# A hybrid attention and state-space block: the first projections with rotations on VectorE, block copies on ScalarE and a reordered softmax

## What is computed

```python
def _compress(k, cmp_idx, pe, w1, w2):
    blk = k[:, cmp_idx] + pe[:, None, :]      # 31 overlapping blocks of 32 tokens
    return jax.nn.silu(blk @ w1) @ w2
q, kc, vc, ks, vs, kw, vw, gates, z = jnp.split(h @ w_in, splits, axis=-1)
s_c = jnp.einsum('bqgrd,bngd->bgrqn', qb, k_cmp) - slopes * (tf - cmp_center)
p_c = _masked_softmax(s_c, cmp_end <= t)      # 0 where a token sees no block
o_c = jnp.einsum('bgrqn,bngd->bqgrd', p_c, v_cmp)
```

## Time and profile before

| | us |
|---|---|
| median of 3 runs | 2048.51 (2045.93 to 2049.92) |
| the profiled execution | 2053.18 |
| its span | 2051.4 |
| busy: TensorE, VectorE, ScalarE, GpSimd | 1826.9, 1005.5, 816.8, 303.3 |
| TensorE's chain share | 66% |

### The profile page before, as it was taken

One profiled execution on the slowest core, in us unless ns is written; L12 is line 12 of the kernel. 1 busy time (PEld: TensorE's weight loads), 2 busy tenths in 40 slices (PEclk: granted clock), 3 DMA queues, 4 the chain that ended last, 5 costly groups with the idle time before them and its releaser, 6 DMA issues.

```text
span 2051.4 us, 23580 instructions
## 1 busy us (share of the span) xinstructions
PE 1826.9 (89%) x9454; PEld 1450.1 (71%) x9454; DVE 1005.5 (49%) x1694; ACT 816.8 (40%) x1348; POOL 303.3 (15%) x376
## 2 busy tenths in 40 slices
PE   3488699997996999999799999999999969999996
PEld 2366578775775787786487777887777748888885
DVE  7647845665564446434434454445544364334323
ACT  4034356763313424333425545256632443223222
POOL 1347432546000000000000000012200021111000
PEclk9789799998998999999999999999999979999998
DMA  3154231005667422321032221321122212233231
GB/s 108 47 168 144 99 98 42 12 1 157 156 157 167 132 84 92 105 95 48 21 116 78 82 83 62 100 69 61 63 82 92 83 41 93 92 103 100 85 95 59
DMA packets 79230, 183.37 MB, mean 89 GB/s; under 512 B 24449, under 2 KB 35585, under 8 KB 77329
## 3 DMA queue, kind: packets, MB, share of 16 engines
q1 hardware_dynamic: 79120, 181.87, 28.7%
HBM read 165.58 MB, written 16.25 MB: 89 GB/s over the span
## 4 chain that ended last, share of the span: by engine, by line
PE 66%; DVE 17%; ACT 8%; DMA 4%; issue 2%; POOL 2%; SPq 1%; DVEq 0%; ACTq 0%; POOLq 0%
PE bank L822 16%; PE bank L823 16%; PE bank L824 15%; DVE wlo L1720 2%; PE bank L861 2%; PE bank L862 2%; PE bank L863 2%; PE bank L1003 2%; PE bank L981 2%; ACT whi L1249 1%; POOL Ps L2473 1%; ACT Ps L1619 1%; DVE Pb L1842 1%; DVE CA L1688 1%; PE bank L842 1%
## 5 line engine op out<-in xcount | busy, mean ns | idle before, releaser
L1720 DVE TENSOR_TENSOR wlo<-wraw,whi 128x1024 fp32r<-128x1024 f32 (+1 forms) x262 | 327.5, 1253 | 344.1 <-ACT whi L1249 342.7
L822 PE MATMUL bank<-Hh,whi 128*128 128x512 f32 (+2 forms) x1136 | 461.2, 406 | 24.0 <-DVE wlo L1720 13.2
L823 PE MATMUL bank<-Hl,whi 128*128 128x512 f32 (+2 forms) x1136 | 448.6, 395 | 0.0
L824 PE MATMUL bank<-Hh,wlo 128*128 128x512 f32 (+2 forms) x1136 | 448.2, 395 | 0.0
L1249 ACT ACTIVATE whi<-wraw 128x1024 fp32r<-128x1024 f32 (+1 forms) x262 | 271.1, 1040 | 373.0 <-PE bank L824 260.1
L822 PEld LDWEIGHTS bank<-Hh,whi 128*128 128x128 f32 (+2 forms) x1136 | 215.5, 190 | 84.5 <-DVE qs L1786 11.8
L824 PEld LDWEIGHTS bank<-Hh,wlo 128*128 128x128 f32 (+2 forms) x1136 | 215.3, 189 | 48.9 <-issue 0.6
L823 PEld LDWEIGHTS bank<-Hl,whi 128*128 128x128 f32 (+2 forms) x1136 | 215.8, 190 | 47.5 <-issue 2.7
L2466 POOL TENSOR_SCALAR bs<-dist 128x256 f32<-128x256 f32 x16 | 7.3, 457 | 831.8 <-DMA dist<-in_c_dist 831.1
L822 PE MATMUL bank<-Bh,whi 128*128 128x512 f32 x256 | 103.1, 403 | 2.2 <-DVE Bl L2244 2.2
L824 PE MATMUL bank<-Bh,wlo 128*128 128x512 f32 x256 | 102.1, 399 | 0.0
(11 more groups left out here) (368 smaller groups left out, 3044.7 us busy)
## 6 DMA issues: line engine op xcount, KB each, us to landing
wraw<-in_w_o SPq DMA_DIRECT2D x24, 512.0 KB, 3.5
wraw<-in_w_bgate SPq DMA_DIRECT2D x24, 512.0 KB, 3.4
wraw<-in_w_branch SPq DMA_DIRECT2D x24, 512.0 KB, 3.5
wraw<-in_w_fg SPq DMA_DIRECT2D x22, 512.0 KB, 3.4
wraw<-in_w_fu SPq DMA_DIRECT2D x22, 512.0 KB, 3.4
wraw<-in_w_s SPq DMA_DIRECT2D x16, 512.0 KB, 4.1
wraw<-in_w_glu SPq DMA_DIRECT2D x16, 512.0 KB, 3.6
wraw<-in_w_fd SPq DMA_DIRECT2D x16, 512.0 KB, 3.5
```

The source lines that it names most:

```text
L822: pe.matmul(o, wh[:, cols], hi(k), start=k == 0, stop=False)
L823: pe.matmul(o, wh[:, cols], lo(k), start=False, stop=False)
L824: m = pe.matmul(o, wl[:, cols], hi(k), start=False, stop=k == K - 1)
L1720: dve.tensor_tensor(c.wlo[q][:, 0:n], c.raw[i % RR][:, 0:n], c.whi[q][:, 0:n].bitcast(F32), S_).then_inc(*up(DID, ("wlo", i)))
```

## The change

- The low part becomes a step of its own, `split_lo`. Up to the end of the projections it stands one use later than the high part; afterwards directly behind it.
- The norm's scale of tile k+1 stands ahead of the low part of tile k. The parameter work of the S5 preparation that stood ahead of and in the norm moves behind it (its parts 3 and 4 are now wider operations in place of many), and the two sines move from among the squares to behind the evictions of `w_kvc` 0 and 1.
- The evictions of `w_kvc` become plain copies on ScalarE. The position vector takes the unused column 31 of the blocks, goes through the same matmul, and returns as a bias in `cmp_hid`.
- Rotations run whole (128x1152 and 128x1024) and all on VectorE; GpSimd keeps memsets and the copies of `pr`. The copies to `Bd` go to ScalarE.
- Order of tiles: `w_kvc`, `w_gate`, then `w_ksw` 0 to 3, each followed by two pieces of `cmp_w1`, then `w_q` 0, 4, 1, 5, 2, 6, 3, 7, then `w_vsw`. The softmax runs per head index r as soon as tiles r and r+4 are there, in two steps (`soft_in`, `soft_out`) with ScalarE's exponential between; its mask product and its floor at 1e-30 go, and the gate is multiplied by `valid` once.
- The stores of `CA`, `K` and `WT` move to later steps. The wait for the last store of `WT` moves from GpSimd to the first writers of `pT`.

```diff
+        lows = deque()
+
+        def low(upto):
+            while lows and lows[0] <= upto:
+                i = lows.popleft()
+                out.append(("split_lo", i))
+                rawuser[i % RR] = -1
...
-                        rawuser[split % RR] = -1
+                        lows.append(split)
...
                         seen = i
+                        low(i + 1)
                         pump(i + LOOK)
+                        low(i)
+                        if not late:
+                            low(i + LOOK)
+                            pump(i + LOOK)
...
+        self.tick()
+        self.step("vecs")
+        for k in range(KT + 1):
+            if k < KT:
+                self.sq.take(("n0", k))
             self.step("norm0", k)
...
+            if k < KT:
+                self.sq.give(("n0", k))
+        self.step("pump", LOOK)
+        self.pair([("w_kvc", 0), ("w_kvc", 1)], "h0")
+        for n in range(2):
+            self.evict(("w_kvc", n))
+        self.tick(2)
+        for n in range(2, 4):
+            self.filled("w_kvc", n, 4)
+        self.filled("w_gate", 0, 4, M=48)
...
+            self.filled("w_ksw", t, 4)
+            if t == 0:
+                self.bank.take("gateT")
+                self.step("gate_t")
+                self.bank.give("gateT")
+            if t == 2:
+                self.cmp_out(0)
+            i, m = t // 2, t % 2
+            if m == 0:
+                self.bank.take(("hid", i))
+            for hf in range(2):
+                j = self.piece("cmp_w1", (i, m, hf), 0, 1024, split=False)
+                self.step("cmp_w1", i, m, hf, j)
+                self.tick()
+            if m == 1:
+                self.step("cmp_hid", i)
+                self.bank.give(("hid", i))
+        self.step("cmp_in")
+        for n, t in enumerate(self.turns):
+            self.filled("w_q", t, 2)
+            if n == 0:
+                self.cmp_out(1)
+            self.compressed(n)
         for j, key in enumerate(self.tok("w_vsw", 0, 512, 2, "h0", self.between_pieces())):
+            if j == 0:
+                self.prep_turn(3, 1)
+                self.step("store_w", 3, 1)
             self.evict(key)
-        self.drain()
         self.step("cmp_end")
+        self.step("first_over")
...
+    turns = (0, 4, 1, 5, 2, 6, 3, 7)
+
+    def filled(self, w, col, n, M=128):
...
-        for part in range(11):
+        for part in range(9):
             self.step("prep", part)
             yield
         for b in range(4):
             self.step("prep_b", b)
             yield
-            for n in range(6):
-                self.step("prep_ca", b, n)
-                yield
-            self.step("prep_neg", b)
-            if b < 3:
-                self.step("prep_in", b + 1)
-            yield
-            if b:
-                self.prep_turn(b - 1, 1)
-                yield
-            for n in range(6):
+            for i in range(2):
+                for n in range(3):
+                    self.step("prep_ca", b, i, n)
+                    if b:
+                        if n == 0:
+                            self.prep_turn(b - 1, i)
+                        elif n == 2:
+                            self.step("store_w", b - 1, i)
+                    yield
+            for n in range(3):
                 self.step("prep_w", b, 0, n)
+                if n == 1:
+                    self.step("store_ca", b)
+                    if b < 3:
+                        self.step("prep_in", b + 1)
                 yield
             self.bank.take(("kk", b))
             self.step("prep_k", b)
             self.bank.give(("kk", b))
-            yield
-            for n in range(6):
+            for n in range(3):
                 self.step("prep_w", b, 1, n)
+                if n == 2:
+                    self.step("store_k", b)
                 yield
-            self.prep_turn(b, 0)
-            yield
-        self.prep_turn(3, 1)
+        self.prep_turn(3, 0)
+        self.step("store_w", 3, 0)
 
     def prep_turn(self, b, i):
         for hf in range(2):
...
+    def compressed(self, n):
+
+        if 1 <= n <= 8:
+            t = self.turns[n - 1]
+            for a in range(2):
+                self.bank.take(("cs", t, a))
+                self.bank.give(("cs", t, a))
+            self.step("cmp_scores", t)
+        if n % 2 == 0 and n >= 4:
+            self.step("soft_out", (n - 4) // 2)
+        if n % 2 == 1 and n >= 5:
+            r = (n - 5) // 2
+            self.bank.take(("ct", r))
+            self.step("cmp_t", r)
+            self.bank.give(("ct", r))
+        if n % 2 == 1 and 3 <= n <= 9:
+            r = (n - 3) // 2
+            self.bank.take(("cq", r))
...
+    def ev_kvc(key):
+        b, n = bank(key), key[1]
+        i, gpair = n // 2, n % 2
+        src = b.rearrange("p (n q two) -> p two q n", q=8, two=2)
+        on.wait_ge(*at("tile", key))
+        on.wait_ge(*at("blk_pe", i))
+        for a in range(2):
+            for par in range(2):
+                for hf in range(2):
+                    x = copy(c.blk[i][par * 64:par * 64 + 64, hf * 8:hf * 8 + 8, :].rearrange(
+                        "p q (g n) -> p q g n", g=4)[:, :, 2 * gpair + a, 0:31], src[a * 64:a * 64 + 64, par, :, hf:hf + 31])
+        x.then_inc(*up(DID, ("blk", i, gpair), ("freed", key)))
...
     def cmp_hid(i):
+        b = bank(("hid", i))[:, 0:256].rearrange("p (m n) -> p m n", m=2)
         on.wait_ge(*at("hid", i))
-        act.activation(c.hid[:, i, :, :].rearrange("p a b -> p (a b)"), bank(("hid", i))[:, 0:256], ACT.Silu).then_inc(
-            *up(DID, ("hid_s", i), ("freed", ("hid", i))))
+        copy(c.hb[:, i, :], b[:, :, 31]).then_inc(*up(DID))
+        on.wait_ge(*now(DID))
+        for m in range(2):
+            x = act.activation(c.hid[:, i, m, :], b[:, m, :], ACT.Silu, bias=c.hb[:, i, m:m + 1])
+        x.then_inc(*up(DID, ("hid_s", i), ("freed", ("hid", i))))
 
...
+    def prep_b(b):
+        on.wait_ge(*at("Bb", b))
+        on.wait_ge(*at("Bd0"))
+        if b:
+            on.wait_ge(*at("kk", b - 1))
+        for i in range(2):
+            for h in range(2):
+                half = slice(h * 64, h * 64 + 64)
+                x = copy(c.Bd[half, i, :, h * 16:h * 16 + 16], c.Bb[half, i, :, :])
+        x.then_inc(*up(DID, ("Bd", b)))
...
-        if part == 1:
+        if part == 2:
             on.wait_ge(*at("angle"))
...
+        if k:
+            s = c.sq[plan.sq.of["n0", k - 1]]
+            hi, lo = c.moving["h0"]
+            on.wait_ge(*at("hi", "h0", k - 1))
+            dve.tensor_tensor(lo(k - 1), s, hi(k - 1).bitcast(F32), S_).then_inc(
+                *up(DID, ("lo", "h0", k - 1), ("freed", ("n0", k - 1))))
...
     def gate_t():
+        b = bank("gateT")[:, 0:192].rearrange("p (j h) -> p j h", j=4)
         on.wait_ge(*at("gateT"))
-        dve.tensor_copy(c.gate[:, :, :].rearrange("p a b -> p (a b)"), bank("gateT")[:, 0:192]).then_inc(
-            *up(DID, ("gate0",), ("freed", "gateT")))
+        on.wait_ge(*at("valid"))
+        dve.tensor_tensor(c.gate[:, :, 0:16], b[:, :, 0:16], c.valid.unsqueeze(2).broadcast_to([128, 4, 16]), M).then_inc(
+            *up(DID))
+        dve.tensor_copy(c.gate[:, :, 16:48], b[:, :, 16:48]).then_inc(*up(DID, ("gate0",), ("freed", "gateT")))
...
+    def rotated(o, x, w, n, y, i, b, step, *names):
+
+        p8 = slice(8 * b, 8 * b + 8)
+        wk = lambda m: w[:, m, 0:n, p8].rearrange("p k q -> p q k").unsqueeze(3).broadcast_to([128, 8, n, 16])
+        yk = lambda m: y[:, m, :, :].unsqueeze(2).broadcast_to([128, 8, n, 16])
+        if step == 0:
+            tt(o, yk(0), wk(i), M)
+        elif step == 1:
+            tt(x, yk(1), wk(1 - i), M)
+        else:
+            tt(o, o, x, A_ if i else S_, *names)
+
+    def prep_ca(b, i, n):
+        if n == 0 and i == 0:
             on.wait_ge(*at("Cq", b))
             if b:
                 on.wait_ge(*at("CAd", b - 1))
                 on.wait_ge(*at("kk", b - 1))
-        (o, a0, a1, op) = c.rotate(c.tA, c.pw, 9, c.Cq, 0, c.CA[:, 0, :, :, :], b, n)
-        tt(o, a0, a1, op, *([("CA_re", b)] if n == 5 else []))
+        o, x = c.CA[:, i, :, :, :], c.tA[:, :, :, :]
+        if (i, n) == (1, 2):
+            on.wait_ge(*now(DID))
+            dve.scalar_tensor_tensor(o, o, -1.0, x, M, S_).then_inc(*up(DID, ("CA", b)))
+        else:
+            rotated(o, x, c.pw, 9, c.Cq, i, b, n)
...
+    def nsa_in():
+        on.wait_ge(*at("cmp_pe"))
+        on.wait_ge(*now(DID))
+        for i in range(2):
+            gp.tensor_copy(c.blk[i][:, :, 31], c.pe2[:, i, :]).then_inc(*up(DID, ("blk_pe", i)))
+        on.wait_ge(*at("total", "x"))
+        gp.memset(c.Kp[:, :, 0:8, :], 0.0).then_inc(*up(DID, ("Kp0",)))
+
+    def prep(part):
+        if part == 5:
+            on.wait_ge(*at("pw"))
+            for k in range(8):
+                x = gp.tensor_copy(c.pr[:, :, k, :], c.pw[:, :, 7 - k, :])
+            x.then_inc(*up(DID, ("pr",)))
 
```

(17 more changed lines are left out.)

335 lines of the change are left out of this document (121 added, 214 removed).

## The result

The changed kernel takes 1978.86 us (median of 4 runs, 1975.99 to 1980.06) where the kernel before, on the same chip, takes 2047.66: ratio 0.966, 95% interval 0.9645 to 0.9674. I had forecast 1982.0, in a range from 1969 to 2010.

What follows compares the result with a forecast made beforehand. VectorE, slowed by GpSimd working beside it, was taken to make TensorE wait in the first 277 us. Phase end 198.3 against 276.9 gave 78.6, less 12 for late hand-overs: gain 66 to 67 from 2048.5, so 1982 us, range 1969 to 2010.

Steps and rivals of the forecast that it cites:

- The unit prices: First phase, operation times without GpSimd beside VectorE: rotations 1.36 and 1.23 us, low parts 1.2, ScalarE block copies 0.33.
- The head: Kernel start to 49.5 us: norm at 17.3, gain 9.3; then TensorE stalls about 11.7 us before `w_kvc` 3.
- The chain: TensorE's work and stalls from 49.5 us to the phase's end at 198.3, against 276.9 before: difference 78.6.
- the 12 I allowed: Allowance for late hand-overs between engines: 0.65 us on each of 18 tiles after 49.5 us, 12 us.
- (b): Four `cmp_w1` blocks and three `w_ksw` tiles: 38.0 us plus stalls 2.4, 1.6, 0.3 and 1.6; 43.9, to 113.6.
- (a): From 49.5 to 69.7 us: `w_kvc` 3 with slow matmuls 7.3, gates 5.5, `w_ksw` 0 with `prep_k` 7.4.
- (c): Eight `w_q` and four `w_vsw` tiles, scores and softmax transposes: 84.7 us, to 198.3, VectorE's 70 us covered.
- (A): Rival, lockstep: VectorE one tile behind among `w_q` and `w_vsw`, 11.3 us a tile for 7.1; time 2028, half 2005; chance 0.13.
- the near tie: From `w_q` 5 to `w_q` 7, VectorE and TensorE both need about 7.5 us a tile.
- (B): Rival, slow clock: TensorE at 1.2 GHz from 49.5 to 113.6 us adds 20 us, time 2002; chance 0.09.
- (C): Rival: rotations slow by form, not through GpSimd, 3.06 and 2.72 us each; time 2059, slower; chance 0.02.
- (D): Rival: stalls only moved, a late load stops TensorE as before, gain within 0.2%; chance 0.02.

Runs made afterwards that it cites:

- low parts early: Changed kernel with each low part directly behind its high part on VectorE's queue, instead of one use later: 1977.4 us, ratio 0.9665.
- both GpSimd runs: Kernel before with GpSimd's rotations cut to one column: 2016.9 us; changed kernel with unused GpSimd products beside VectorE's rotations: 1998.8 us.
- D: Changed kernel with sine ahead of the pair, tile 3's parts early, first `prep_k` later, four low parts straight behind evictions: 1955.3 us, ratio 0.9555.

## Why the prediction was right, and where it was off

**The unit prices** held within 2%: rotations 1.358 and 1.225 us for 1.36 and 1.22, low parts 1.220, block copies 0.324 in a row (5.19 for 16) for 0.33. (`Bd`, which had no price, took 0.310.) The reason given for them, that the slow rows were those with GpSimd at work, is shown from both sides. What I had missed is its form: an operation of one engine waits for a part of the other's, so a wide one loses no more than a narrow one.

**The head** came as written: inverse 17.2 (17.3), norm 17.4 (17.3), first matmul 19.8 (19.5), pair's end 32.3 (32.3), copies 37.0 (37.3), sine 38.6 (39.0), TensorE again at 49.2 (49.5) after 11.35 us (11.7). As a description it was right, but for one sum: 5.3 us of copies from 0.7 us before the pair's end give 36.9, not the 37.3 that it used. As an account of worth it was not right: what the norm gained by the parameter work's leaving the head (5.3 us), the sine's late place took back and more (9.1).

**The chain** ends at 198.3 and the phase ended at 204.6, so the lateness was 6.3 us and not the 12 I allowed, which put the end at 210. That is the mis-sized term. The 12 was worked out from no row: I took the stalls of (b), 1.5 us on average, and chose less than half of them for every tile. By parts: 0.3 early at 49.2; (a) 21.2 us for 20.2; (b) 47.0 for 43.9; (c) 87.2 for 84.7. In (c) no further weight tile waits at all, so "a little late at every tile" was the wrong picture; lateness sits at the four `w_ksw` waits, 7.2 us where I had 5.9, and in the clock behind two of them. After the wait that ends at 76.91, twelve matmuls took 4.4 us for 2.8, and `w_q` 0 behind 117.4 took 7.2 for 5.6, together 3.2 of the 6.3:

```profile
78.00:80.00 2.00, 2.00 (x6) 1.52 (x6) 1.73 (x7) 0.00 (x0) 0.00 (x0) 0.50 0.82 250
...
120.00:122.00 2.00, 2.00 (x6) 1.55 (x5) 1.97 (x2) 0.14 (x1) 0.00 (x0) 0.50 1.04 391
```

**The rest of the program** took 1774.3 us before and 1772.5 and 1769.3 in two executions after; the 0.5 us at attention's start can't be read from that. The phase's 72.5 us and the 66.8 to 72.7 of the interval of the ratio fit each other; my 66.6 lies just below its lower end, by the allowance.

**Rivals.** (A), lockstep: not there, and with low parts early no tile fell behind either, so the near tie was none. (B), the slow clock: in part, one spell of some 4 us in (b) and one at the start of (c) beside the one that I counted, not all of (a) and (b). (C): refuted by 1.358 us, and by both GpSimd runs. (D): refuted.

**Table load and copies.** The table load starts 0.01 us behind the copy and the sine 1.29 us later, with no time for a drain between, so the row of before was a better guide than the Trainium skill's drain ("ScalarE: Activation LUTs", section "What ACT_TABLE_LOAD costs"). Nor do the copies from PSUM bear out the 1.6 that I had drawn from the Trainium skill's "Perfetto Trace Analysis", section "Engine Utilization": plain copies of 64x248 took 0.32 to 0.37 us on ScalarE and, in the variant with the block copies on VectorE, 0.41 there.

**What stays open.** The first `cmp_w1` load no longer makes TensorE wait, but no run took that reordering of tiles or of stores back alone, so its share of the 72.5 us (21.1 us of wait before) is argued and not shown. What GpSimd's own lateness, apart from contention, cost the kernel before is not shown either. D's remaining waits (6.0 us for low parts) were not tried.

## To carry to other kernels

Before giving GpSimd a share of VectorE's elementwise work, look at what VectorE's neighbours cost in the stretches where both run; operations of the two on SBUF took turns here, and each cost VectorE 0.5 to 0.8 us on top of its own time. A small step at the head of a long chain (here one sine) can matter more than a large one elsewhere: follow each long wait back over all queues until an engine was idle for something that could have been issued earlier. And count a wait of TensorE with the slow matmuls behind it, for shortening several waits a little gave more than their sum.
